# First block of a two-block transformer: w_ada sums on TensorE between GEMMs by halves, on one Trainium2 core

## The reference, cut to what matters

```
mod = silu(c) @ w_ada + b_ada            # 1 x 3072, w_ada is 1024 x 3072
shift, scale, gate = split(mod, 3)       # 1024 each
h = rms_norm(x, norm_g) * (1 + scale) + shift
z = h @ w_in                             # 1024 x 2976: c_q, c_kv, k_rope | g_mla | q_b | k_b | v_b | g_moba
o_mla  = mla_attention(rms_norm(c_q) @ w_uq, rms_norm(c_kv) @ w_ukv, k_rope)
o_moba = moba_attention(q_b, k_b, v_b)   # 8 heads each, causal
x = x + gate * (concat(silu(g_mla) * o_mla, silu(g_moba) * o_moba) @ w_out)
```

## Time and profile before

| what | value |
|---|---|
| median of 3 runs | 1709.75 us (1706.80 to 1710.27) |
| profiled execution: its own time, span | 1710.25 us, 1708.4 us |
| PE busy | 1602.2 us (94%) |
| DVE busy | 1068.1 us (63%) |
| ACT busy | 854.1 us (50%) |
| DMA share of the first twentieths of the span | 0.9, 0.5, 0.7, 0.5 of 16 engines |
| first matmul of the first GEMM | at 60.2 us |
| end of the first block | at about 386 us |

### The profile page before, as it was taken

How to read it: one execution, slowest core, us unless ns; L and a number is a source line. 1 busy time by engine, 2 the same in 40 slices (tenths; PEclk the granted TensorE clock), 3 DMA queues, 4 the chain that set the end, 5 groups by cost and what they waited for, 6 DMA issues and landing times.

```text
span 1708.4 us, 21793 instructions
## 1 busy us (share of the span) xinstructions
PE 1602.2 (94%) x7796; PEld 1318.6 (77%) x7796; DVE 1068.1 (63%) x1792; ACT 854.1 (50%) x1487; POOL 121.9 (7%) x157
## 2 busy tenths in 40 slices
PE   1769989999999999999999999999999999999998
PEld 1557768777888777878778887888878787778886
DVE  5787677666565646567675556565565567665653
ACT  0346536645444555555464445444465655454442
POOL 3011001100000200002100000000020001200000
PEclk9998989999999999999999999999999999999999
DMA  9575257335555563455655555555582453655552
GB/s 279 202 241 188 72 183 232 128 111 182 188 186 191 149 189 117 124 149 158 193 186 184 189 192 177 187 180 197 161 222 87 130 173 117 210 182 189 177 192 76
DMA packets 155336, 293.27 MB, mean 172 GB/s; under 512 B 10214, under 2 KB 23316, under 8 KB 155228
## 3 DMA queue, kind: packets, MB, share of 16 engines
q1 hardware_dynamic: 149312, 276.60, 50.1%
q0 software_dynamic: 4800, 12.29, 3.2%
q10 hardware_dynamic: 1116, 2.99, 0.5%
HBM read 290.77 MB, written 1.06 MB: 171 GB/s over the span
## 4 chain that ended last, share of the span: by engine, by line
PE 79%; DVE 8%; DMA 5%; ACT 3%; issue 3%; POOL 1%; SPq 0%; DVEq 0%; POOLq 0%; ACTq 0%
PE pb L433 75%; PE pb L437 4%; DMA raw<-in_w_in 3%; DVE wl L1290 2%; DVE acc L1287 1%; DMA raw<-in_w_ada 1%; POOL st L2041 1%; ACT wh L803 1%; DVE xt_l L1287 1%; ACT xt_h L803 1%; DVE dg L1284 0%; ACT pb L803 0%; DVE xt_l L1290 0%; DVE h L1287 0%; DVE pb L1293 0%
## 5 line engine op out<-in xcount | busy, mean ns | idle before, releaser
L803 ACT ACTIVATE wh<-raw 128x1024 fp32r<-128x1024 f32 (+1 forms) x484 | 504.9, 1053 | 440.0 <-PE pb L433 375.9
L1290 DVE TENSOR_TENSOR wl<-raw,wh 128x1024 fp32r<-128x1024 f32 (+1 forms) x484 | 579.2, 1216 | 208.0 <-ACT wh L803 204.3
L433 PE MATMUL pb<-wh,xt_h 128*128 128x512 f32 (+2 forms) x1536 | 593.4, 386 | 14.2 <-ACT wh L803 12.2
L433 PE MATMUL pb<-wl,xt_h 128*128 128x512 f32 (+2 forms) x1536 | 585.4, 381 | 19.0 <-DVE wl L1290 18.9
L433 PE MATMUL pb<-wh,xt_l 128*128 128x512 f32 (+2 forms) x1536 | 585.6, 381 | 0.6 <-DVE xt_l L1287 0.4
L433 PEld LDWEIGHTS pb<-wl,xt_h 128*128 128x128 f32 x1536 | 292.1, 190 | 73.9 <-DVE wl L1290 23.9
L433 PEld LDWEIGHTS pb<-wh,xt_h 128*128 128x128 f32 x1536 | 291.8, 190 | 70.5 <-ACT xt_h L803 12.8
L433 PEld LDWEIGHTS pb<-wh,xt_l 128*128 128x128 f32 x1536 | 291.5, 190 | 59.4 <-DVE xt_l L1287 6.5
L433 PE MATMUL pb<-wh,big_h 128*128 128x512 f32 x352 | 138.7, 394 | 0.0
L433 PE MATMUL pb<-wl,big_h 128*128 128x512 f32 x352 | 138.6, 394 | 0.0
L433 PE MATMUL pb<-wh,big_l 128*128 128x512 f32 x352 | 136.7, 388 | 0.0
(11 more groups left out here) (205 smaller groups left out, 1479.0 us busy)
## 6 DMA issues: line engine op xcount, KB each, us to landing
raw<-in_ffn_w_gu SPq DMA_DIRECT2D x176, 512.0 KB, 4.5
raw<-in_w_in SPq DMA_DIRECT2D x148, 512.0 KB, 4.3
raw<-in_ffn_w_down SPq DMA_DIRECT2D x88, 512.0 KB, 3.8
raw<-in_w_ada SPq DMA_DIRECT2D x48, 512.0 KB, 5.5
raw<-in_w_out SPq DMA_DIRECT2D x32, 512.0 KB, 4.0
raw<-in_w_branch SPq DMA_DIRECT2D x24, 512.0 KB, 3.6
raw<-in_w_in SPq DMA_DIRECT2D x8, 416.0 KB, 4.0
G<-in_na_rpb POOLq DMA_DIRECT2D x32, 96.0 KB, 8.5
```

The lines of the kernel that those rows point to most:

```text
L433: return e.matmul(o, a, b, start=start, stop=stop)
L803: return e.activation(o, a, func, **kw)
L1290: return e.tensor_tensor(o, a, b, op)
```

## The change

All of it lies in the first block.

- Of the four tiles that the first GEMM needs, (0, 2) and (0, 3), and only these, are computed by TensorE: `ada_row` multiplies the 128 x 1 column of silu(c) by the raw chunk, two float32 matmuls of 512 columns, into one row of bank 7. ScalarE copies the row out (`row_out`), and `turn_both` turns it together with the tile that VectorE has summed.
- x is turned, scaled and shifted in halves of four column groups. z and qb are each run as two parts by halves of their sum (`part=0` and `part=1`): the first parts need only shift and scale of the first 512 columns, tiles (0, 0) and (0, 2). The order becomes: x first half, z part 0, half of the next two tiles, qb part 0, the other half, x second half, z part 1, qb part 1. Layer 1 has the same order with tile (1, 3) between; this tile was in layer 0's output GEMM.
- The remaining tiles are bound to regions: two beside q1 to gmla ("lat"), two gate tiles beside gmoba, (1, 2) beside layer 0's output; in layer 1 (1, 4) beside q1 to gmla and (1, 5) beside gmoba. None is beside qb, kb and vb of layer 0.
- VectorE keeps chunks of w_ada in a queue of its own, `weights`. It sums one after the attention's steps of each chunk, and earlier only those whose buffer the stream needs.
- `acc` has three buffers (the third is `dg`). Steps of x take pairs of column groups (512 wide), and one half of the rows is scaled by ScalarE.
- The broadcast vectors `bc` are loaded by SyncE from chunk 36 on, not by GpSimd at the start; constants and row vectors are loaded in parts; the angle reduction stands in the start; the heads of q are turned inside vb, q0 runs before the heads of k are turned; the norms of z, qb and kb are steps of `side`, with z's sum of squares on ScalarE.

```diff
+    side_tiles = {("lat", 0): [(1, 0), (1, 1)], ("gmoba", 0): [(0, 4), (0, 5)], ("out", 0): [(1, 2)],
+                  ("lat", 1): [(1, 4)], ("gmoba", 1): [(1, 5)], ("out", 1): []}
...
+        def ada_row(l, j, kq):
+
+            c = ada_chunk(l, j, kq)
+            v = chunk_view(raw[c % NRAW], c)
...
+            for k in range(2):
+                kx = 2 * kq + k
+                last = mm(banks[7][0:1, :], stat(8, "c_silu")[:, kx:kx + 1], v[:, k, :], kx == 0, kx == 7)
+            last.then_inc(*up("row", l, j, kq))
...
+        for kq in range(4):
+            ada_chunk(0, 0, kq)
+            ada_row(0, 2, kq)
+            if kq == 1:
+                b = rot("cols")
+                w.wait_ge(*at("rows"))
+                tr(b[:, 0:126], rows[0:126, :]).then_inc(*up("rtr"))
+            if kq == 2:
+                take_early(("z", 0), win, 0, 416, [(0, 2)])
+        take_early(("z", 0), win, 0, 416, [(2, 2)])
+        take_early(("qb", 0), win, 928, 512, [(0, 2), (2, 2)])
+        turn_x(0, 0)
+        turn_both(0, 0, 2)
+        gemm(("z", 0), XT, 0, xkey0, win, 0, 416, "eva", part=0)
+        for kq in range(2):
+            ada_chunk(0, 1, kq)
+            ada_row(0, 3, kq)
+        gemm(("qb", 0), XT, 0, xkey0, win, 928, 512, "eva", part=0)
+        for kq in range(2, 4):
+            ada_chunk(0, 1, kq)
+            ada_row(0, 3, kq)
+            if kq == 2:
+                turn_x(0, 4)
+        take_early(("z", 0), win, 0, 416, [(4, 2), (6, 2)])
+        turn_both(0, 1, 3)
...
+            if l:
+                turn_x(l, 0)
+                later.drain()
+                later.add((ada_chunk(1, 3, kq) for kq in range(4)), 4)
+                later.over(4)
+                gemm(("z", l), XT, 0, xkey, win, 0, 416, "eva", part=0)
+                turn_x(l, 4)
+                gemm(("qb", l), XT, 0, xkey, win, 928, 512, "eva", part=0)
+                turn_row(1, 3)
+            gemm(("z", l), XT, 0, xkey, win, 0, 416, "eva", part=1)
...
+        def split(chunks):
+
+            for c in chunks:
+                if plan[c][5]:
+                    weights.append(c)
+                else:
+                    lower_part(c)
+            i = min(stream.taken + AHEAD, len(split_at) - 1)
+            while weights and weights[0] <= split_at[i] - NRAW + 1:
+                weigh(weights.popleft())
...
                 for _ in group:
+                    later.fill()
                     side.fill()
-                    later.fill()
+                    weigh_one()
```

More of the change, by code:

```diff
@@ L123, in add @@
     def add(self, steps, n):
[L124 to L125 removed]
+        if n:
+            self.todo.append([steps, n])
+            self.left += n
     def over(self, chunks):
@@ L200, in take, with groups @@
         return due
-def groups(nk, n, head, tail):
+def groups(nk, n, head, tail, part=None):
     per = 1024 // n
     chunks = [(c0, min(per, nk - c0)) for c0 in range(0, nk, per)]
+    if part is not None:
+        m = len(chunks) // 2
+        return [[c] for c in (chunks[m:] if part else chunks[:m])]
     tail = min(tail, len(chunks) - head)
@@ L608, in pe, with xkey0, turn_x @@
         tr(b[:, 0:8], rows[0:8, :]).then_inc(*up("ctr"))
[L609 to L616, removed]
+        def xkey0(t, kx):
+            return ("x", 0), kx | 1
+        def turn_x(l, c0):
+            to_xt(("x", l), lambda c, t: xn[:, t, c * 128:c * 128 + 128], c0 + 4, lambda c, t: [(f"xn{t}", l)], by="xm", c0=c0)
+        win = d["w_in"][0]
+        for kq in range(4):
[23 more added lines that the diff above has]
+        turn_both(0, 1, 3)
         ps, pts = Ring(pb1), Ring(pt1)
@@ L661, in pe @@
             side.over(4)
+            more("gmoba", 4)
             gemm(("gmoba", l), XT, 0, xkey, win, 2464, 512, "evd")
@@ L668, in pe @@
                 w.wait_ge(*at("acc", l, 4 + j2, 7))
-                mm(o, ones, acc[ada_no[l, 4 + j2] % 2][:, :], True, True).then_inc(*up("turn", l, 4 + j2))
+                w.wait_ge(*at("cst"))
+                mm(o, ones, acc[acc_no[l, 4 + j2] % 3][:, :], True, True).then_inc(*up("turn", l, 4 + j2))
             side.drain()
-            later.add((None for _ in range(4)), 4)
-            later.add(ada(side_tiles[l, 1]), 5 * len(side_tiles[l, 1]))
-            later.over(8)
+            more("out", 8)
             to_xt(("o", l), lambda c, t: ob[:, t, c * 128:c * 128 + 128], 8, lambda c, t: [("sgo", l, t)])
@@ L805, in take @@
         def take():
-            for c in stream.take():
+            split(stream.take())
+        def split(chunks):
+            for c in chunks:
                 src, kk, n, _, i, ada_ = plan[c]
@@ L827, in temp, with gemm @@
             return v
[L829 to L832, removed]
+        def gemm(g, x, nk, n, evac, head=1, tail=1, between=None, mid=None, part=None):
+            if not part:
+                pair_no[0] += 1
+                bank_of[g] = 2 * ((pair_no[0] - 1) % 2)
+            first_bank = bank_of[g]
+            gs = groups(nk, n, head, tail, part)
             for gi, group in enumerate(gs):
@@ L961, in act, with rows_squares @@
         ac_(stat(8, "c_t"), cols[:, 0:8], ACT.Tanh, scale=0.5).then_inc(*up("ctanh"))
[L962 to L966, removed]
+        load_rows(rows_in[1:])
         rot()
-        def rows_norm(l, ready):
+        def rows_squares(l, ready):
             for t in range(2):
@@ new lines, in act, with row_out @@
+        rows_squares(0, lambda t: ("x",))
+        e.dma_start(mq[0:32, 0, 0:512], d["consts"][0:32, C_OH:C_END]).then_inc(*landed("oh"))
+        def row_out(l, j):
+            w.wait_ge(*at("row", l, j, 3))
+            ac_(row_sum(l, j), banks[7][0:1, :]).then_inc(*up("sum", l, j))
+        rows_scale(0)
+        split(stream.lead(9))
+        for a0, a1 in ((C_CAUS, C_INV), (C_ZERO, C_OH)):
+            e.dma_start(cst[:, a0:a1], d["consts"][:, a0:a1]).then_inc(*landed("cst"))
+        row_out(0, 2)
@@ L982, in act @@
+        first = turn_x(0, 0)
+        next(first)
+        split(stream.lead(1))
+        next(first)
+        rot()
+        split(stream.lead(2))
+        split(stream.lead(8))
+        row_out(0, 3)
+        second = turn_x(0, 4)
+        split(stream.lead(1))
+        next(second)
+        split(stream.lead(1))
+        next(second)
+        rot()
         ps, pts, pt_read = Ring(pb1), Ring(pt1), {}
         for l in range(NL):
-            if l:
-                rows_norm(l, lambda t: ("hn", ("b1", 0), t, 512))
@@ L986, in act, with more @@
[L986 to L997, removed]
+            def more(region, chunks):
+                later.drain()
+                later.add(ada(side_tiles[region, l]), 5 * len(side_tiles[region, l]))
+                later.over(chunks)
@@ L1560, in reduce_angle, with weigh_next @@
                 *up("angle", which))
+        def weigh_next(n):
+            for c in stream.lead(n):
+                weigh(c)
+        weigh_next(2)
+        w.wait_ge(*at("pos"))
+        e.tensor_copy(stat(2, "pos"), posi[:, :]).then_inc(*up("posf"))
+        w.wait_ge(*at("posf"))
+        w.wait_ge(*at("inv"))
+        for t in range(2):
+            ts(ang[:, 0, t * 16:t * 16 + 16], cst[:, C_INV:C_INV + 16], stat(2, "pos")[:, t:t + 1], None,
+               ALU.mult, None).then_inc(*up("ang0", t))
+        rows_var(0)
+        weigh_next(2)
+        rows_scale(0)
+        reduce_angle(0)
+        b = rot()
+        w.wait_ge(*at("rtr"))
+        e.tensor_copy(cols[:, 8:126], b[:, 8:126]).then_inc(*up("cols"))
+        weigh_next(2)
+        reduce_angle(1)
+        early = stream.lead(1)
+        weigh_next(2)
+        split(early)
+        first = turn_x(0, 0)
+        next(first)
+        turn_both(0, 0, 2)
+        factors(0, 0)
+        next(first)
+        split(stream.lead(1))
+        next(first)
+        split(stream.lead(2))
+        weigh_next(8)
+        second = turn_x(0, 4)
+        next(second)
+        turn_both(0, 1, 3)
+        factors(0, 1)
+        next(second)
+        split(stream.lead(1))
+        next(second)
+        split(stream.lead(1))
         def rope1(v, nh, t, key):
@@ L1604, in dve @@
[L1604 to L1616 removed]
+                factors(l, 0)
@@ new lines, in dve @@
+                rows_var(l)
+                weigh_one()
+                rows_scale(l)
+                for _ in turn_x(l, 0):
+                    pass
+            gemm(("z", l), XT, 8, 416, nothing, part=0)
+            second = turn_x(l, 4)
+            if l:
+                next(second)
+            gemm(("qb", l), XT, 8, 512, nothing, part=0)
+            if l:
+                turn_row(l, 3)
+                factors(l, 1)
+                for _ in second:
+                    pass
+            gemm(("z", l), XT, 8, 416, nothing, part=1)
@@ L1628, in dve @@
+                yield
+                moba_norm("kb", 512, l)
+                yield
+                yield
+            side.add(norms(), 10)
+            side.over(10)
+            gemm(("qb", l), XT, 8, 512, nothing, part=1)
```

(7 more changed lines are left out.)

426 lines of the change are left out of this document (259 added, 167 removed).

## The result

| | before | after |
|---|---|---|
| median | 1707.87 us (10 runs, 1705.91 to 1711.31) | 1701.13 us (10 runs, 1698.05 to 1707.29) |
| profiled execution, span, clock | 1710.25, 1708.4, 0.989 | 1700.5, 1698.7, 0.979 |

The account below looks back on a forecast made before the run. TensorE bounds the kernel (busy 1602.2 of 1708.4 us), DMA early in the start. Terms -32 + 3.5 + 1.5 + 1 + 1.5 = -24.5 against 1710.25 give 1686 us; forecast 1680 to 1693 (0.46), range 1671 to 1700.

Parts of the forecast that it names:

- Steps 1 to 3: Start to layer 0's first score: first GEMM at 31 us, z part 1 at 58, score at 100; gain 32 us.
- Step 4: Sums moved into the attentions: +3.5 us in layer 0's moba stage (-1 to 7), +1.5 beside gmoba, +1 in layer 1.
- step 2: Start, x's second half: row chunks hold raw buffers until TensorE has passed; z part 1 starts at 58 us.
- the +1.5 of the forecast: Beside gmoba in layer 0: five more sums hidden except the last, a chunk of (1, 2), costing 1.5 us.
- Step 5: Layer 1's start: two chunks of (1, 3) summed after the last residual add; 1.5 us slower, between -2 and 5.
- forecast 1: Layer 1's moba stage: six sums for two, 6 us more VectorE work, costing 1 us.
- B: Rival: low clock and the ring in the start make it 13 us late, 1699 us in all; chance 0.22.
- C: Rival: VectorE becomes the bound in the attentions, each moved sum costing 1.5 us; +6.5, 1717 us; chance 0.07.
- A: Rival: sums fit in VectorE's gaps, clock rises early, step 1 ends at 28 us; -36, 1673 us; chance 0.18.
- a moba stage over 50 us: Sign in layer 0's moba attention that would show the prediction wrong.
- Two signs for it: No DMA standstill before 58 us; VectorE busy over 38 us between first score and the heads of mla.
- TensorE never waited for `acc`: Sign against the prediction: TensorE waiting for `acc` more than twice after the start.

Follow-up runs that it names:

- Experiment 2: The changed kernel, sums of four lat and gmoba tiles reading x's buffer instead of their chunk, so no load buffer is held (true values left out): 1689.52 us.
- experiment 1: The changed kernel, but VectorE sums each w_ada chunk where it is due in the stream, not behind the attention's steps: 1688.12 us.
- experiment 7: The kernel of experiment 1, but q0 runs behind the heads of k again, as in the kernel before: 1693.72 us.
- the last version: The kernel of experiment 1 with layer 1 in whole GEMMs and tile (1, 0) moved beside qb part 1, kb and vb of layer 0: 1688.33 us.
- Experiment 6: The kernel of experiment 1, but tiles (0, 2) and (0, 3) of the start are summed by VectorE again, not TensorE: 1693.57 us.

## Why the prediction missed

**Steps 1 to 3** held: forecast -32, measured -32.9. First GEMM 27.7 for 31, z part 1 53.2 for 58, first score 99.3 for 100. The row chunks cost what was estimated (1.9 and 3.6). The errors of these steps offset each other: the start was 5 us faster, while the time from z part 1 to the score was 46.1 for 42. There z part 1 took 7.9 us for 4.6: TensorE had been idle for 2.4 us before it, waited 0.95 for `wl`, and its matmuls of 416 columns stood 0.35 us apart up to 58.8, the level of 1.2 GHz, and 0.19 from there on. Before the first score came the wait of 3.1 for `kt`. Two small readings were wrong: in the stretch of 365 GB/s not only large transfers were under way (165 of its 447 packets were under 512 B), and the DMA shares in the table of before are those of the first fortieths of the span, 42.7 us each, not twentieths.

**Step 4, the term of +3.5 for the moba stage, is what failed:** it measured +15.5, twice its upper bound of 7. The load was not undercounted: VectorE was busy for 37.8 us where 39.7 was forecast. The step priced a sum by the time that it takes on VectorE, and so took seven us for all of them as the worst case. What a sum costs where it is put off is the buffer that it keeps: step 2 counted this for TensorE's row chunks, and step 4 did not for VectorE's, though "earlier only those whose buffer the stream needs" stood in the change. Experiment 2 takes only the hold away: the stage is then 42.6 us for 38.1, +4.5, where +3.5 was forecast, and it is 34.8 beside gmoba, the +1.5 of the forecast. So the terms that the step had were about right in size, and the hold, which it put at nothing, is 11.0 us here (53.6 less 42.6) and some 2 beside gmoba, which is within what profiles differ by. With each sum at once (experiment 1) it is +7.1 in the stage and -0.6 beside gmoba: the sums then stand ahead of the attention's steps, but hold their buffers less.

**Step 5** forecast +1.5. From the first output transpose to layer 1's first score it was +3.7: 1.1 in the output GEMM, 2.6 from layer 1's start on. TensorE's wait before x is turned is 4.10 us for 2.82. Of the two chunks that the step had between the last residual add and the variance (3.1 us of sums), one stands there, in two instructions:

```profile
217.88 1.53 DVE L1452 SCALAR_TENSOR_TENSOR acc<-raw,st,acc 128x512 f32<-128x512 f32 x2
```

With each sum at once this stretch is +0.4 and the wait 2.83, so this loss came with the deferral too; experiment 2, which frees the buffers of four earlier tiles only, keeps it (+3.4). The moba attention of layer 1 cost 0.4 (forecast 1), the rest of the layer gave 0.7.

**The rivals.** B has nearly the right time (1699) for the wrong reason: the start is not late. Its low clock did come, at the first two row chunks (3.57 and 3.21 us) and in z part 1, but it cost 2 to 3 us beyond the forecast and not 13. C named VectorE's load, which experiments 1 and 2 refute. A's own term of -36 gives 1674, not 1673. Of the signs, a moba stage over 50 us was to show the prediction wrong, and it came true. Two signs for it failed as well: the DMA engines stood nearly still from 51 to 55 us, and VectorE was busy for 37.8 us, not over 38, and 33.8 of them lie between the first score and the first head of mla's q. TensorE never waited for `acc`. The measured excess of the moba stage and beside gmoba is +19.2, the forecast for both +5; this difference of 14.2 is the miss, the errors of the other terms cancel. Without the hold or without the deferral the kernel takes 1689.5 or 1688.1, for a forecast of 1686. That these are so near is in part luck: in experiment 1 the first score is at -31.6, the moba stage costs +7.1, beside gmoba it is -0.6 and the rest of the block costs +1.7, which are not the terms of the sum.

## What to carry to other kernels

Where several consumers share one ring of load buffers, price a consumer that is put off by what its buffer keeps waiting, not by its own length. VectorE had time for the sums (busy for 37.8 of 57.6 us), and putting them off still cost 13 us, through SyncE, a late weight chunk, and an in-order ScalarE that also serves the critical chain. The sign is in the waits: a consumer of loads that had no wait for them gets one (ScalarE, 19.5 us for none), the loading queue has a new releaser (`acc`, 42.7 us for 3.8), the DMA share falls and no engine is full. The releaser alone does not tell the loss: a queue that runs ahead always waits for someone, and in the version with chunks taken two sooner SyncE still waits 33.8 us for `acc` from 100 to 146 us (32.7 in the change), but ScalarE only 6.9 for loads (19.2). Free the shared buffer first; if the work must wait, let it wait on a buffer of its own.

## What was not expected of the hardware

The second block, with the same code, took 1322.9 to 1324.5 us in most of the profiles, but 1328.7 in experiment 7 and 1326.8 in the last version. Of experiments 7 and 1, the timeline of PE at the same operation, and the 10 us from it:

```profile
595.23 0.92 PE L446 MATMUL pb<-cst,A 128*128 128x128 f32 x4 [2.40 <-ACT mqt L891]
```
```profile
595.00:605.00 10.00, 9.78 (x42) 7.46 (x43) 4.08 (x11) 5.88 (x15) 0.00 (x0) 0.83 0.39 131
```
```profile
592.23 0.66 PE L446 MATMUL pb<-cst,A 128*128 128x128 f32 x4 [2.32 <-ACT mqt L891]
```
```profile
592.00:602.00 10.00, 9.77 (x50) 7.33 (x51) 4.71 (x15) 6.45 (x16) 0.00 (x0) 1.00 0.51 169
```

After nearly the same wait, 2.40 and 2.32 us, one goes on at a clock of 0.83 and one at 1.00, and in the same 10 us it gets 42 matmuls done instead of 50. What decides between them stays open. It makes differences of 3 to 5 us between two kernels of this size uncertain, those of experiment 7 and of the last version among them. (Experiment 6's loss is not of this kind: its second block took 1323.0 us.)
